# First group of each expert layer: rows selected for the first expert alone, for the other three during the second expert's gates

## What is computed

```
gsel = argmax(xt @ wg + bg)                      # one of 4 groups
topv, topi = top_k(le[gsel], 2)                  # 2 of the group's 4 experts
gates = softmax(topv) * p_sel                    # spread over 16 experts
hg, hv = split(xt @ w_gate_up[e])                # 2048 -> 2 x 512
act = silu(hg) * hv * gates[e]
out = sum over e of act @ w_down[e]              # 512 -> 2048
x = layer_norm(alpha * x + out)
```

## Time and profile before

| | before |
|---|---|
| median of 3 runs | 1443.62 us |
| profiled execution, whole | 1443.33 us |
| its span, first to last instruction | 1441.2 us |
| TensorE busy (matmul) | 1357.6 us, 94% |
| VectorE, ScalarE, GpSimd busy | 523.6, 365.8, 28.5 us |
| granted TensorE clock, mean | 0.984 of full speed |
| bytes moved by DMA | 489.03 MB |
| chain that ended last | TensorE 69%, DMA 25%, VectorE 3%, ScalarE 2% |

### The profile page before, as it was taken

One profiled execution on the slowest core, in us unless ns is written; L12 is line 12 of the kernel. 1 busy time (PEld: TensorE's weight loads), 2 busy tenths in 40 slices (PEclk: granted clock), 3 DMA queues, 4 the chain that ended last, 5 costly groups with the idle time before them and its releaser, 6 DMA issues.

```text
span 1441.2 us, 20719 instructions
## 1 busy us (share of the span) xinstructions
PE 1357.6 (94%) x9012; PEld 757.9 (53%) x9012; DVE 523.6 (36%) x1081; ACT 365.8 (25%) x564; POOL 28.5 (2%) x38
## 2 busy tenths in 40 slices
PE   8999999999899999999999998899999899889985
PEld 8999999999743333343234226653343243224321
DVE  6877887643332022022004018633042013103303
ACT  5567666433310130021012003420021012002001
POOL 0000001000000000000000000000000000000000
PEclk8999999999899999999999999999999999999998
DMA  9776452844599999999999988689999999999993
GB/s 302 234 215 187 139 184 81 277 170 176 179 386 406 428 409 428 427 427 428 427 426 429 427 344 328 233 286 366 427 428 425 428 427 427 426 427 428 426 427 127
DMA packets 94566, 489.03 MB, mean 339 GB/s; under 512 B 8408, under 2 KB 64664, under 8 KB 67320
## 3 DMA queue, kind: packets, MB, share of 16 engines
q1 hardware_dynamic: 89536, 468.61, 81.7%
q10 hardware_dynamic: 2266, 10.27, 2.2%
q0 software_dynamic: 2672, 8.82, 1.6%
HBM read 481.95 MB, written 16.04 MB: 346 GB/s over the span
## 4 chain that ended last, share of the span: by engine, by line
PE 69%; DMA 25%; DVE 3%; ACT 2%; issue 1%; ACTq 0%; DVEq 0%; POOL 0%; SPq 0%; POOLq 0%
DMA ring<-in_moe_w_down 23%; PE ps L1285 19%; PE ps L1264 17%; PE ps L1032 5%; PE ps L1034 5%; PE ps L1033 5%; PE ps L1183 5%; PE ps L1120 2%; PE ps L1122 2%; PE ps L1121 2%; PE ps L1207 1%; PE ps L1348 1%; ACT xtok L668 1%; DVE xsel L1989 1%; DMA xtok<-in_x_prompt 1%
## 5 line engine op out<-in xcount | busy, mean ns | idle before, releaser
L1264 PE MATMUL ps<-ring,xsel 128*64 128x512 f32 x2016 | 452.2, 598 | 28.1 <-DMA ring<-in_moe_w_gate_up 27.2
L1285 PE MATMUL ps<-ring,work 128*32 128x512 f32 x3072 | 342.9, 594 | 16.6 <-DMA ring<-in_moe_w_down 16.6
L1264 PEld LDWEIGHTS ps<-ring,xsel 128*64 128x64 f32 x2016 | 138.0, 137 | 315.3 <-issue 259.9
L1285 PEld LDWEIGHTS ps<-ring,work 128*32 128x32 f32 x3072 | 93.8, 110 | 233.9 <-issue 210.4
L1881 DVE SCALAR_TENSOR_TENSOR arena<-arena,ps 64x512 f32<-64x512 f32 x32 | 21.7, 678 | 480.6 <-ACT work L882 480.6
L1032 PE MATMUL ps<-operands,whi 128*128 128x288 f32 x512 | 152.6, 298 | 0.0
L1034 PE MATMUL ps<-operands,ring_lo 128*128 128x288 f32 x512 | 152.1, 297 | 0.0
L1033 PE MATMUL ps<-ring_lo,whi 128*128 128x288 f32 x512 | 151.5, 296 | 0.0
L1423 DVE TENSOR_TENSOR ring_lo<-ring,whi 128x1024 fp32r<-128x1024 f32 x96 | 115.8, 1221 | 58.7 <-ACT whi L684 58.4
L684 ACT ACTIVATE whi<-ring 128x1024 fp32r<-128x1024 f32 x96 | 100.6, 1058 | 129.5 <-PE ps L1034 72.5
L881 ACT ACTIVATE arena<-ps 64x512 f32<-64x512 f32 x32 | 18.9, 590 | 394.5 <-PE ps L1264 394.5
(11 more groups left out here) (360 smaller groups left out, 1170.5 us busy)
## 6 DMA issues: line engine op xcount, KB each, us to landing
ring<-in_moe_w_gate_up SPq DMA_DIRECT2D x126, 2048.0 KB, 21.0
ring<-in_moe_w_down SPq DMA_DIRECT2D x64, 2048.0 KB, 22.3
ring<-in_lru_w_in SPq DMA_DIRECT2D x15, 2048.0 KB, 10.1
ring<-in_lru_w_out SPq DMA_DIRECT2D x8, 2048.0 KB, 12.0
x_rows<-xtok ACTq DMA_DIRECT2D x4, 1024.0 KB, 3.9
xtok<-in_moe_w_gate_up SPq DMA_DIRECT2D x2, 2048.0 KB, 12.6
ring<-in_pool_w SPq DMA_DIRECT2D x4, 1024.0 KB, 13.7
xtok<-in_x_prompt SPq DMA_DIRECT2D x2, 1024.0 KB, 8.0
```

Of the source, the lines that this page charges most:

```text
L1264: last = mm(ps[half * ES:(half + 1) * ES, e % 2, :], xsel[:, k, e * ES:(e + 1) * ES], wt[:, half * 512:(half + 1) * 512], start=(k == 0), ...
L1285: last = mm(ps[rows:rows + QB, 2 + r, :], act[:, e % 2, f * W + slots0:f * W + slots0 + QB], wt[:, d * 512:(d + 1) * 512], start=start, st ...
```

## The change

The first window's `select_rows` selects for expert 0 alone (64 moving columns instead of 256, and evacuations of 64). The other three experts' rows are selected by eight new pairs of matmuls with 192 moving columns each, `select_rest(q)`, placed at parts 14, 16, ... 28, into PSUM banks 2 and 3. ScalarE evacuates all eight (`rest_rows`): pair 0 before the copy of the turned `sel`, pairs 1 to 3 after the first expert's tanh and copy, pair 4 after the first activations' copy, 5 to 7 after the copy of the places. The gates of expert 1 wait for them pair by pair. The product of `sel` and the gates goes into a buffer of its own, `first_sel`, and VectorE's choice for the next window waits until all eight new pairs were made.

```diff
+REST_AT = {14 + 2 * q: q for q in range(PAIRS)}
...
+        first_sel = carve(work, 3584, NE, ES)
...
+                def rest_rows(parts):
+                    for q in parts:
+                        eng.wait_ge(rest_turned, PAIRS * l + q + 1)
+                        for b in range(2):
+                            k = 2 * q + b
+                            last = eng.activation(xsel[:, k, ES:NE * ES], ps[:, 2 + q % 2, b * 192:(b + 1) * 192], ACT.Identity,
+                                                  scale=affine_of[:, l, 0, k:k + 1], bias=affine_of[:, l, 1, k:k + 1])
+                        last.then_inc(rest_ready, 1)
...
-                def even_rows(w, q):
+                def even_rows(w, q, n=NE):
...
-                        last = eng.activation(xsel[:, k, :], ps[:, 6, b * 256:(b + 1) * 256], ACT.Identity,
+                        last = eng.activation(xsel[:, k, 0:n * ES], ps[:, 6, b * 256:b * 256 + n * ES], ACT.Identity,
...
+                    if first:
+                        rest_rows(range(0, 1))
                     eng.wait_ge(act_turned[l], w * (NE + 1) + 1)
...
+                        if first and e == 0:
+                            rest_rows(range(1, 4))
                         eng.wait_ge(act_turned[l], w * (NE + 1) + (e + 2))
                         eng.activation(act[:, e % 2, :], ps[:, 6 + e % 2, 0:KF * W], ACT.Copy).then_inc(act_ready[l], 1)
                         if e == 0 and first:
+                            rest_rows(range(4, 5))
                             eng.wait_ge(places_done, l + 1)
                             eng.activation(places_raw, ps[:, 5, RAW_AT:RAW_AT + WINS * W // 4], ACT.Copy).then_inc(places_out, 1)
+                            rest_rows(range(5, PAIRS))
                         if e == 0 and first and l == 1:
                             eng.wait_ge(slots_full, 3 * l + 3)
...
-                    even_rows(0, q)
+                    even_rows(0, q, 1)
...
+                def select_rest(q):
+                    for b in range(2):
+                        last = mm(ps[:, 2 + q % 2, b * 192:(b + 1) * 192], row_block(2 * q + b),
+                                  sel[0:W, 1:NE, :].rearrange("p e j -> p (e j)"), start=True, stop=True)
+                    last.then_inc(rest_turned, 1)
...
-                        last = mm(ps[:, 6 + q % 2, b * 256:(b + 1) * 256], XS.rearrange("s (c p j) -> s c j p", c=4, j=4)[:, k // 4, k % 4, :],
-                                  sel[0:W, :, :].rearrange("p e j -> p (e j)"), start=True, stop=True)
+                        last = mm(ps[:, 6 + q % 2, b * 256:b * 256 + n * ES], row_block(k),
+                                  sel[0:W, 0:n, :].rearrange("p e j -> p (e j)"), start=True, stop=True)
...
+                        weighted = first_sel if first else sel
...
-                                select_rows(w, r)
+                                select_rows(w, r, 1 if first else NE)
+                        if first and i in REST_AT:
+                            select_rest(REST_AT[i])
...
+                            if first and e == 1 and k % 2 == 0:
+                                eng.wait_ge(rest_ready, PAIRS * l + k // 2 + 1)
...
-                    TT_(sel[0:W, :, :], sel[0:W, :, :], gslot[0:W, :].unsqueeze(2).to_broadcast([W, NE, ES]), ALU.mult)\
-                        .then_inc(sel_ready[l], 1)
+                    TT_((first_sel if first else sel)[0:W, :, :], sel[0:W, :, :],
+                        gslot[0:W, :].unsqueeze(2).to_broadcast([W, NE, ES]), ALU.mult).then_inc(sel_ready[l], 1)
...
+                            if first:
+                                eng.wait_ge(rest_turned, PAIRS * (l + 1))
                             choose(lk, slot_rank[0:W, bass.ds((w + 1) * NE, NE)])
```

More of the change, by code:

```diff
@@ L394, in encoder_step @@
         pool_diff = sem("pool_diff")
+        rest_turned, rest_ready = sem("rest_turned"), sem("rest_ready")
         out_st = sem("out_st")
@@ L1172, in turn_places, with row_block, select_rows @@
                     last.then_inc(slots_full, 1)
-                def select_rows(w, q):
+                def row_block(k):
+                    return XS.rearrange("s (c p j) -> s c j p", c=4, j=4)[:, k // 4, k % 4, :]
+                def select_rest(q):
[3 more added lines that the diff above has]
+                    last.then_inc(rest_turned, 1)
+                def select_rows(w, q, n=NE):
                     if q == 0:
@@ L1198, in turn_spread @@
                     def turn_spread():
+                        weighted = first_sel if first else sel
                         for e in range(NE):
-                            last = nc.tensor.transpose(ps[0:ES, 7, e * W:(e + 1) * W], sel[0:W, e, :], ident[0:W, 0:W])
+                            last = nc.tensor.transpose(ps[0:ES, 7, e * W:(e + 1) * W], weighted[0:W, e, :], ident[0:W, 0:W])
                         last.then_inc(act_turned[l], 1)
@@ L1784, in put_to, with odd_rows @@
                     ins.then_inc(dst_ready[l], 1)
-                def odd_rows(w, q):
+                def odd_rows(w, q, n=NE):
                     eng.wait_ge(rows_turned[l], w * PAIRS + (q + 1))
@@ L1789, in odd_rows @@
                         k = 2 * q + b
-                        ins = TS_(xsel[:, k, :], ps[:, 7, b * 256:(b + 1) * 256], affine_of[:, l, 0, k:k + 1],
+                        ins = TS_(xsel[:, k, 0:n * ES], ps[:, 7, b * 256:b * 256 + n * ES], affine_of[:, l, 0, k:k + 1],
                                   affine_of[:, l, 1, k:k + 1], ALU.mult, ALU.add)
@@ L1922, in moe @@
                 for q in range(1, PAIRS, 2):
-                    odd_rows(0, q)
+                    odd_rows(0, q, 1)
                 for w in range(FLAT):
```

## The result

The changed kernel takes **1461.4 us** (median of 4 runs, 1456.57 to 1464.03), against 1443.47 us for the kernel before in the same comparison (4 runs, 1442.95 to 1444.52): ratio **1.011**, 95% interval 1.0091 to 1.0129, 18 us slower. The forecast was 1451.1 with a range up to 1454.2: right in direction, too small by more than half. The profiled execution took 1462.53 us, with a span of 1460.4.

A forecast was written before the change was run, and what follows sets the result against it. The weight stream bounds most of each expert layer, TensorE the first group's head. Net TensorE 9.4 - 4.3 = +5.1 us in layer 0, +2.7 in layer 1: 1443.33 + 5.1 + 2.7 = 1451.1 us, range 1443.5 to 1454.2.

The forecast's parts named there:

- The bound, and where lateness goes: Layer 0's first-group head: TensorE alone bounds it, and its time is handed to the weight stream one for one, +5.1 us.
- Chunk 13's issue: Layer 0's weight transfer at part 31: issued 5.1 us later, 48 us after the landing, with a wider hole before it.
- Chunk 12's: Layer 0's weight transfer at part 23: issued at an unchanged 34.3 us after the landing, 4.3 saved against five pairs added.
- a narrow group of eight costs between 0.96 and 1.11 us: First selections at 64 columns: taken as 1.05 us against 2.17, so three groups save 3.4 us.
- the start: First selection pair and the two evacuations behind it, after the rows land: 0.9 us saved.
- Rival (b): Early slots make the stream gain if a 192-column pair costs streaming alone, 0.64 us: 1439.7 us; chance 10%.
- The pairs: Eight 192-column pairs at parts 14 to 28: five at 1.29 and three at 1.0 add 9.4 us, upper bound 9.8.
- Layer 1: Late norm rows and chunk 13 rest the stream; 3.8 us behind at 302 of 429 GB/s loses 2.7 us.
- The norm rows: Layer 1's two closing-norm row transfers on ScalarE's queue: issued behind pair 7's evacuation, 6 to 7 us later.
- (a): Rival for both layers: full slots in reserve cover the added 5 us; 1443 to 1445 us, chance 13%.
- (c): Rival in layer 0: ScalarE evacuates each pair late, seven pairs by 1 us on top; about 1458 us, chance 5%.
- (d): Rival at the head: first gates wait for something else, no early start; 1452 to 1453 us, inside the forecast's 72%.

The follow-up runs named there:

- half the dose: Four extra 192-column pairs (parts 14, 18, 22, 26), results unused, added to the first group of the kernel before: 1452.83 us, ratio 1.005.
- Runs 6 and 9: Changed kernel with contiguous stationary blocks: 6 by ScalarE writing the rows permuted, 1454.1 us; 9 by the PSUM addresses the transposes write, 1447.37 us.
- run 4: The changed kernel measured once more, unchanged, against the kernel before: 1461.24 us, ratio 1.0104.
- run 11: The changed kernel with layer 1's two norm-row transfers issued on ScalarE before the evacuation of pair 7 instead of behind it: 1462.81 us, ratio 1.0114.

## Why the prediction was wrong, point by point

**The bound, and where lateness goes: right.** The head is TensorE's alone, and layer 0 hands its lateness to the end nearly one for one (10.67 of 10.72 us; 4.99 of 5.19 at half the dose; with contiguous blocks 5.01 and 2.39 of 4.12). Chunk 13's issue slipped as described, from 43.0 to 53.7 us after the landing (48 had been forecast), and the stream's hole grew to 6 us. Chunk 12's did not keep its distance from the landing: 41.2 us, not 34.3. By the prediction's own terms the five pairs ahead of it (5.9 us) already outweighed the 4.3 saved, by 1.6; it counted 1.5 in layer 1 and nothing in layer 0. Measured, 0.9 was saved, the pairs and their cuts took 6.2, and the clock 1.6.

**The step that failed: "a narrow group of eight costs between 0.96 and 1.11 us".** It measured 2.01, so the three groups saved 0.5 us and not 3.4, and the start 0.4 and not 0.9 (the first pairs and the evacuations, 2.51 to 2.08). Of the 4.3 us that were to come back, 0.9 did. The nearest rows had been taken by shape alone (128 columns of weights, few moving ones: 0.12 us each), and in one of them (lines 1221 to 1228) the stationary columns lie side by side, in the other (line 1207) they are every second, at the same 188 to 192 ns a load. Here they are every fourth. Such a load has a floor of 2.01 / 8 = 0.25 us an instruction, which a 256-column matmul (0.27 with all around it) nearly hides and a 64-column one cannot. Runs 6 and 9, which changed the addresses, gave 1.03. At half the granted clock (run 4) the narrow strided group takes 2.06 us, hardly more, so that it is not TensorE's streaming that holds it. The floor stood in the trace of before: its loads of line 1183 have a mean of 327 ns, those of line 1207 192. The prediction took its load times from TensorE's steps in the chain and not from the weight-load rows.

The Trainium skill, "TensorE: Matmul & The Clock Gate", section on LDWEIGHTS, gives a load as its columns by 1.2, whatever its rows: 107 ns for 128. In this case's weight-load rows even the contiguous load is longer, 188 to 192 ns. The layout of the columns in memory is not in that rule, and here it moved the load from about 190 to 327 ns. The prediction's "the 0.12 us of the narrow rows agrees" compared the rule with a step of the chain, and only for columns side by side. Rival (b), built on that rule, failed by the measured pair: 1.18 us, not 0.64.

**The pairs: right.** 7 x 1.18 + 1.01 = 9.3 us with about 0.15 for each of five cuts: 10.0 against 9.4. The bound of 9.8 was slightly passed for the same reason as above: a pair is 0.85 with contiguous blocks.

**A term that was missing: the clock.** In each head of the three profiled runs with the change's layout and narrow selections (the change twice, and run 11; six of six) the granted clock fell after the landing, though TensorE was busy throughout, for 1.6 us of TensorE time in layer 0 (4.17 - 2.73 and 0.64 - 0.44) and 3.3 in layer 1 of the change. None of the twenty other heads has it. Of those, twelve have wide matmuls with strided blocks, four wide ones with contiguous blocks and four narrow ones with contiguous blocks, so the fall came only with narrow matmuls and dear loads together. Why this pattern lowers the clock no run tested.

Per head the terms add up: 10.0 + 1.6 - 0.9 = 10.7 measured in layer 0, and with 3.3 for the clock 12.4 in layer 1 (12.34).

**Layer 1: the direction of the mechanism right, its arithmetic wrong.** The norm rows move while TensorE holds up chunk 13, and the change does issue them late: 51.7 us after the landing in place of 38.5, where 6 to 7 us more had been forecast. The loss was forecast as a rate over a stretch. What fits the runs better is the lateness less about 3.7 us, near the lead of the rows. At +5.1 us of lateness this would give 1.4, not 2.7; at the real 12.34 it gives 8.6 (8.54 measured). Against the profiled run the forecast was 11.4 us short: 5.6 in layer 0's head, 7.2 in layer 1's, less 1.4 for this step. The relation was found with the profiled runs of the table and was not tried with rows issued much sooner, so that the cause of what layer 1 swallows is argued and not shown.

**The rivals.** (a) falls for the change: with strided blocks at most 0.4 us was swallowed in layer 0, and in layer 1 3.4 to 5.1 us, a part of the change's 12.34. (b) falls. (c) falls: the change's chain has no step of ScalarE between the landing and the first down product, and the evacuations of 192 columns took 507 ns, as costed. (d) did happen in part: the first gates began 0.4 us sooner instead of 0.9, for the price of the load and not for another wait.

**The range** reached the upper bounds of every term as it had them. It failed because the narrow group lay 0.9 us above its upper bound, three times a head, and because nothing stood for the clock.

## What to carry to other kernels

Before a matmul is split or made narrower, read its own weight-load rows, not only the matmul's: here the stationary operand's address stride (every fourth 4-byte value) set a floor, and moving 64 columns in place of 256 saved 0.16 us of 2.17. Work that is added at the head of a stream, where each transfer waits for a slot, can be handed to the end nearly whole (layer 0), while the same work in a group that waits for its weights later cost 2 us where it had cost 17. Another transfer that can fill the gap may take part of it back; in layer 1 some 3.4 to 5.1 us went that way, as far as single executions tell. And look at more than one execution before a difference of 1 or 2 us in a stage is given a cause.

## What the runs showed of the hardware

- A load of 96 x 128 4-byte values whose columns are every fourth took 324 to 327 ns in the trace, with contiguous columns 189 to 191. Every second column was as cheap as contiguous ones: 192 to 193 ns for 64 x 128. The load's effect in the chain: 2.01 to 1.03 us for eight narrow instructions, 2.17 to 1.92 for eight of 256 columns.
- At half the granted clock (0.50) eight narrow strided instructions took 2.06 us against 2.01 at full clock, while eight and twelve gate matmuls around them, partly in the lower clock, took 2.79 against 1.89 and 4.14 against 2.73.
- ScalarE writing 128 x 512 with every fourth address: 1216 ns against 777. Transposes of TensorE writing permuted addresses of PSUM cost nothing that shows: they took 274 ns in the mean, against 272 to 346 before, and ScalarE's 776 ns are those of before.
- The granted clock fell behind narrow strided matmuls in six heads of six, and in none of twenty others. It cost 1.6 or 1.7 us in each layer 0, and 3.3, 4.0 and 5.3 in layer 1 (a head's growth less the 9.1 us of its other terms).
- While the two row transfers spread over 96 partitions were moved, the DMA engines were at full share and moved 252 to 285 GB/s for 8 us, against 427 in the weight stream.
